# Norms walked by token halves: the third and fourth block ahead of each norm and the first two behind it, with all squares added on VectorE

## The chip, the cores and the metric

One core of a Trainium2 chip runs the whole program. The metric is the device time of one execution in microseconds (us). PE is TensorE, ACT ScalarE, DVE VectorE, POOL GpSimd, SP the engine whose queue issues the DMAs.

## What is computed

Two kinds of transformer layers in fp32: two layers of a first kind (attention with a pair of softmaxes, a pool mixer, a convolution, SwiGLU) and one layer of a second kind (latent attention beside a gated recurrence, SwiGLU). Each normalises 512 latent tokens and 256 context tokens of 1024 features before its input projection, and the residual again before its feed-forward part. For this case only this skeleton matters (cut from the reference):

```python
for l in range(DEPTH):                                   # 2
    h = modulate(rms_norm(x, norm1_g[l]), sh1, sc1)      # 512 tokens
    hc = modulate(rms_norm(xc, norm1_g[l]), csh1, csc1)  # 256 tokens
    ...
    x = x + g1 * jnp.einsum('blm,md->bld', mix, w_out[l])
    x = x + g2 * swiglu(modulate(rms_norm(x, norm2_g[l]), sh2, sc2), w_ffn_in[l], w_ffn_out[l])
    ...                                                  # xc likewise, in layer 0 only
# the second kind, one layer, on x and a new context ctx
h = modulate_2(rmsnorm(x, g_norm_mix[layer]), sh1, sc1)
hc = modulate_2(rmsnorm(ctx, g_norm_mix[layer]), csh1, csc1)
...
x = x + gt1 * mix_lat
x = x + gt2 * swiglu_2(modulate_2(rmsnorm(x, g_norm_ffn[layer]), sh2, sc2), w_gate[layer], w_up[layer], w_down[layer])
return rmsnorm(x, g_final)
```

with `rms_norm(x) = x * rsqrt(mean(x*x) + eps) * g` and `modulate(h) = h * (1 + scale) + shift`. The shifts, scales and gates come from a vector times w_mod.

## The kernel before

**Layout.** x lies in SBUF as 8 feature tiles of 128 partitions, each with 768 tokens (512 latent, then 256 context); layers 1 and 2 need only the 512 after their input projection. Every weight matrix is walked in blocks of 256 output columns, that is two output tiles. A block is numbered n through the whole program: per layer 10 or 14 input blocks (`base_in[l]`), 4 output blocks (`base_out[l]`), then the feed-forward part (`base_ffn[l]`) in groups of 6, 6, 6 and 4 up blocks, each group followed by 4 down blocks.

**A block.** SP loads its weights into one of two slots (`raw`, n % 2), once POOL has split block n-2. ACT copies the high part (`split_hi`, 1.9 us for 8 tiles), once PE is through with block n-2, and POOL subtracts to get the low part (`split_lo`, some 5 us, semaphore `lo_ready`). PE then makes three products per feature tile (high by high, high by low, low by high) of 128 x 128 weights with 512 tokens, and again with 256 context tokens in layer 0. Block n writes one half of PSUM, n % 2. For one block behind each norm there is a third place for the weights (`early_hi`, `early_lo`, 7 of its 8 tiles), so that its split needn't wait for PE.

**A norm.** There are seven, numbered ni = 0 to 6: before the input projection (even) and before the feed-forward part (odd) of layers 0, 1 and 2, and the final one (6). Norms 0, 2 and 4 are over 768 tokens, 1 too, the others over 512. Around norms 1 to 6 the four blocks ahead (output or last down blocks) add to x: DVE adds a tile's products (`add_to_x`), ACT squares the tile (`norm_square`), DVE adds the square to `n_acc` (`norm_add`, `NORM_ADDED` = 5 of them; the last two squares are summed by PE). PE then sums over the partitions by products with a column of ones (`token_columns`), ACT takes the root, DVE inverts it and spreads it to `n_wide`, PE transposes that into PSUM. Then tile by tile: DVE multiplies (`xg`), ACT adds the shift and rounds to the high part (`h_hi`), DVE makes the low part (`h_lo`, semaphore `n_h`). The first block behind the norm takes its 8 feature tiles in that order, waiting for each.

**Other work in between.** Modulation vectors are made in 12 pairs per layer, spread over earlier blocks (`place`, `pair_in_block`): 8 or 16 steps on DVE (`pair_halves`, half before the block's own work and half in the block before), then sums or transposes on PE at the end of the block (`then` in `products`, lines 2494 and 2507), and SP loads the next pair when one is saved. Each engine's order is the order written in its function; nothing is planned at run time.

The lines behind the steps: 2542 are the products of most blocks, 1162 and 1182 those of layer 2's input projection, 684 the column sums, 2483 a norm's transposes, 2836 those of the output, 2151 makes `xg`, 2138 `h_lo`, 1855 `h_hi`, 1788 splits the high part, 1680 the low part, 2174 a modulation step.

## Time and profile before

| | |
|---|---|
| median of 3 runs | 2583.73 us (2577.93 to 2584.11) |
| profiled execution: its time / its span | 2577.28 us / 2575.5 us |
| PE busy, share of the span | 2445.3 us, 95% |
| DVE | 1337.2 us, 52% |
| ACT | 798.5 us, 31% |
| POOL | 884.9 us, 34% |
| mean granted clock of PE | 0.966 of full speed |

The profile is of one execution. A line of a timeline gives start and length in us, the engine, the line of the kernel, what is written and read, and in brackets how long the engine had stood idle and what released it. Matmuls are pipelined, so the distance of their starts tells the rate, not their length.

### The profile page before, as it was taken

To read this page: it belongs to the slowest core of one execution; us is meant where nothing else is said; L and a number is where in the kernel's file an instruction comes from. 1 tells how busy PE (TensorE), PEld (TensorE's weight loads), DVE (VectorE), ACT (ScalarE), POOL (GpSimd) and SP (SyncE) were. 2 spreads that over 40 slices of the span, in tenths; PEclk is the share of its full clock that TensorE was granted. 3 is DMA by queue.
4 is the path that set the end of the run, shared out by engine and by line. 5 is a ranking of instruction groups with operands and counts; after the bars stand their busy time and mean duration, and the time that the engine had idled before them with its cause. 6 is when DMAs were issued, how large, how long until landed. Compare 5 with 4: busy or idle time off the path is not lost.

```text
span 2575.5 us, 30755 instructions
## 1 busy us (share of the span) xinstructions
PE 2445.3 (95%) x13017; PEld 2019.1 (78%) x13017; DVE 1337.2 (52%) x1709; ACT 798.5 (31%) x1088; POOL 884.9 (34%) x633
## 2 busy tenths in 40 slices
PE   7999899999999999899999999998999988999998
PEld 3888778788888888778777778877988557888886
DVE  2899766646444343695656655654562424211113
ACT  2222661311211111425732122235343443222222
POOL 2006002223333332365034445543453003454442
PEclk9898899899999999899999999998999999999999
DMA  8332203224334242232034546432113002233331
GB/s 265 95 104 83 66 1 111 70 87 143 99 113 132 82 131 82 65 107 75 1 98 131 149 146 175 151 115 66 50 35 114 17 1 65 70 95 98 90 98 58
DMA packets 309225, 240.57 MB, mean 93 GB/s; under 512 B 10692, under 2 KB 304831, under 8 KB 309087
## 3 DMA queue, kind: packets, MB, share of 16 engines
q1 hardware_dynamic: 308674, 238.47, 30.5%
q8 instruction: 103, 1.69, 0.3%
q14 instruction: 34, 0.28, 0.0%
q10 hardware_dynamic: 414, 0.13, 0.0%
HBM read 232.29 MB, written 2.10 MB: 91 GB/s over the span
## 4 chain that ended last, share of the span: by engine, by line
PE 86%; DVE 9%; ACT 3%; issue 1%; DMA 1%; POOL 0%; SPq 0%; DVEq 0%; ACTq 0%
PE ps L2542 62%; PE ps L1162 5%; DVE mod_w L2174 2%; PE ps L2577 2%; PE ps L946 2%; PE ps L684 2%; DVE mod_ctx L2174 1%; PE ps L733 1%; PE ps L1182 1%; PE ps L2457 1%; PE ps L2494 1%; PE ps L760 1%; DVE small L1050 1%; PE ps L908 1%; ACT probs L990 1%
## 5 line engine op out<-in xcount | busy, mean ns | idle before, releaser
L1680 POOL TENSOR_TENSOR w_lo<-raw,w_hi 128x512 fp32r<-128x512 f32 x518 | 757.2, 1492 | 1380.5 <-ACT w_hi L1788 1380.4
L2542 PE MATMUL ps<-h_hi,w_hi 128*128 128x512 f32 x1994 | 649.4, 372 | 25.2 <-DVE h_lo L2138 21.1
L2542 PE MATMUL ps<-h_lo,w_hi 128*128 128x512 f32 x1994 | 639.5, 367 | 0.0
L2542 PE MATMUL ps<-h_hi,w_lo 128*128 128x512 f32 x1994 | 638.9, 366 | 0.0
L1788 ACT ACTIVATE w_hi<-raw 128x2048 fp32r<-128x2048 f32 (+2 forms) x155 | 264.8, 1708 | 577.3 <-PE ps L2542 365.3
L2542 PEld LDWEIGHTS ps<-h_hi,w_hi 128*128 128x128 f32 x1994 | 340.4, 191 | 93.9 <-issue 23.1
L2542 PEld LDWEIGHTS ps<-h_hi,w_lo 128*128 128x128 f32 x1994 | 339.9, 190 | 67.1
L2542 PEld LDWEIGHTS ps<-h_lo,w_hi 128*128 128x128 f32 x1994 | 340.4, 190 | 65.9 <-issue 0.2
L2065 ACT ACTIVATE xg<-ps 128x512 f32<-128x512 f32 (+1 forms) x66 | 44.2, 670 | 679.4 <-PE ps L2542 492.6
L2174 DVE SCALAR_TENSOR_TENSOR mod_w<-mod_w,cond 128x512 f32<-128x512 f32 x224 | 242.0, 1080 | 3.4
L2542 PE MATMUL ps<-hid_hi,w_hi 128*128 128x512 f32 x704 | 231.7, 370 | 0.0
L2542 PE MATMUL ps<-hid_lo,w_hi 128*128 128x512 f32 x704 | 230.3, 368 | 0.0
L2542 PE MATMUL ps<-hid_hi,w_lo 128*128 128x512 f32 x704 | 230.3, 368 | 0.0
L2423 DVE TENSOR_TENSOR sq<-xg,ps 128x512 f32<-128x512 f32 (+1 forms) x66 | 51.1, 775 | 342.6 <-ACT xg L2065 342.5
L2201 DVE SCALAR_TENSOR_TENSOR x<-ps,modc,x 128x512 f32<-128x512 f32 (+1 forms) x160 | 100.6, 678 | 208.1 <-PE ps L2542 208.1
L2542 PEld LDWEIGHTS ps<-hid_hi,w_lo 128*128 128x128 f32 x704 | 120.4, 188 | 24.6
L2542 PEld LDWEIGHTS ps<-hid_lo,w_hi 128*128 128x128 f32 x704 | 120.5, 188 | 24.3
L2542 PEld LDWEIGHTS ps<-hid_hi,w_hi 128*128 128x128 f32 x704 | 120.5, 188 | 24.0
L2426 DVE TENSOR_TENSOR hid_lo<-sq,hid_hi 128x512 fp32r<-128x512 f32 (+1 forms) x66 | 90.2, 1367 | 85.8 <-ACT hid_hi L2068 85.8
L1087 DVE SCALAR_TENSOR_TENSOR conv_acc<-u_conv,col_b,conv_acc 128x783 f32<-128x783 f32 (+1 forms) x120 | 123.6, 1030 | 4.2
L2174 DVE SCALAR_TENSOR_TENSOR mod_ctx<-mod_w,cond,mod_ctx 128x512 f32<-128x512 f32 x112 | 108.3, 967 | 0.0
L1162 PE MATMUL ps<-h_hi,w_hi 128*128 128x512 f32 (+1 forms) x196 | 73.3, 374 | 0.9 <-POOL w_lo L1680 0.9
(380 smaller groups left out, 3225.8 us busy)
## 6 DMA issues: line engine op xcount, KB each, us to landing
mod_w<-in_w_mod SPq DMA_DIRECT2D x72, 1024.0 KB, 9.6
raw<-in_w_ffn_in SPq DMA_DIRECT2D x88, 512.0 KB, 5.3
raw<-in_w_in SPq DMA_DIRECT2D x54, 512.0 KB, 4.9
raw<-in_w_ffn_out SPq DMA_DIRECT2D x48, 384.0 KB, 3.8
raw<-in_w_out SPq DMA_DIRECT2D x24, 512.0 KB, 4.6
raw<-in_w_gate SPq DMA_DIRECT2D x22, 512.0 KB, 4.0
raw<-in_w_up SPq DMA_DIRECT2D x22, 512.0 KB, 5.4
raw<-in_w_down SPq DMA_DIRECT2D x24, 384.0 KB, 3.8
```

What stands on the lines that cost most here:

```text
L684: ins = pe.matmul(ps[:, at + j:at + j + 1], square[:, P * j:P * j + P], ones[:, 0:1], start=first and j == 0, stop=last, skip_group_check= ...
L946: ins = pe.matmul(ps[:, PV2_AT:PV2_AT + 256], values(us[u]["k0"] // P + k, us[u]["h"]), probs_t[:, k, 256 * (j % 2):256 * (j % 2) + 256], ...
L1087: ins = dve.scalar_tensor_tensor(acc, frm, w, acc, ALU.mult, ALU.add)
L1162: ins = pe.matmul(ps[:, at:at + tw], weight, v[:, k, t0:t0 + tw], start=(k == 0 and r == 0), stop=(k == KD - 1 and r == 2))
L1680: ins = pool.tensor_tensor(w_lo[:, s, at:end], raw[:, s, at:end], w_hi[:, s, at:end].bitcast(F32), ALU.subtract)
L1788: act.activation(w_hi[:, s, 0:floats], raw[:, s, 0:floats], ACT.Copy).then_inc(hi_ready, 1)
L2174: ins = dve.scalar_tensor_tensor(to, w, by, to if step >= chains else mod_bias[:, :, :], ALU.mult, ALU.add)
L2201: ins = dve.scalar_tensor_tensor(xt, ps[:, at:at + tw], modc[:, l % 2, chunk + 2 * b + t, c:c + 1], xt, ALU.mult, ALU.add)
L2423: dve.tensor_tensor(ffn_h[:, s, 0:T], ffn_sg[:, s, 0:T], ps[:, 2048 * s + 1024:2048 * s + 1024 + T], ALU.mult).then_inc(psum_free[s], 1)
L2426: dve.tensor_tensor(hid_lo[:, i, 0:T], ffn_h[:, s, 0:T], hid_hi[:, i, 0:T].bitcast(F32), ALU.subtract).then_inc(f_lo, 1)
L2542: ins = pe.matmul(ps[0:m, at:at + tw], weight(part, k, cols), v[:, held[k] if held else k, t0:t0 + tw], start=(at_k == 0 and j == 0 and no ...
L2577: ins = pe.matmul(ps[:, first + width * t:first + width * (t + 1)], v[:, k, rows], w[:, k, :], start=(k == 0 and j == 0), stop=(k == KD - ...
```

## The change

For norms 1, 2, 3, 5 and 6 the tokens are divided in two halves: 512 and 256 where there are 768 (norms 1 and 2), 256 and 256 otherwise. The first two blocks ahead of the norm stay whole. PE walks the third and fourth in six parts and two: third block's half 0 (both output tiles), fourth block's half 0, fourth block's half 1, third block's half 1; the norm's sums and transposes of half 0 lie between the last parts. The first two blocks behind norms 1, 3 and 5 are walked half 0 of both, then half 1 of both. The sums of half 1 stand in the first block behind the fifth feature tile, for norm 2 too. DVE adds, squares are summed and tiles are made half by half in an order written out in `late_adds`. All 7 additions of squares are made on DVE, so that PE sums one column per 128 tokens instead of three.

Norm 4 is done differently: its 256 context tokens don't change in layer 1, so their half is squared, summed and normed within layer 1's last group of up blocks (`CTX_BLOCK` and the two behind it); the 512 latent tokens follow where the norm was, and PE starts layer 2 with the context tokens of its first two blocks. Norm 6's output is turned and stored in two halves.

The places that go with it: the early weight buffers are now whole and serve the first block behind norms 1, 2, 3 and 5 (before: the second; at norm 4 still the second); the second block's high split stands on ACT between two squares of half 1; layer 2's modulation pairs sit one block later; `pool_wt` moves into memory behind the early buffers and is cleared once more by POOL in layer 1.

```diff
-EARLY = 7 * 256
+EARLY = 2048
...
-        place([(2, p) for p in range(12)], [base_ffn[1] + 1 + 3 * p for p in range(12)])
+        place([(2, p) for p in range(12)], [base_ffn[1] + 2 + 3 * p for p in range(12)])
...
-        early_blocks = [n for l in range(3) for n in ([base_in[l] + 1] if l else []) + [base_ffn[l] + 1]]
-        NORM_ADDED = 5
+        early_blocks = [base_ffn[0], base_in[1], base_ffn[1], base_in[2] + 1, base_ffn[2]]
+        NORM_ADDED = 7
...
+        HALVES = {1: [(0, LAT), (LAT, CTX)], 2: [(0, LAT), (LAT, CTX)], 4: [(LAT, CTX), (0, LAT)]}
+        SPLIT = (1, 2, 3, 5, 6)
...
+        LATE = {(2, 0, 0): 1, (2, 0, 1): 2, (3, 0, 0): 3, (3, 0, 1): 4, (3, 1, 0): 5, (2, 1, 0): 6}
...
+        CTX_BLOCK = base_ffn[1] + 30
...
+            block_ready(n, 0, n // 2)
+            pe.wait_ge(n_h[0], KD * 4 + KD)
+            first_products(wh, wl, 0, 1024, LAT, CTX)
+            norm_sums(4, 1)
+            first_products(wh, wl, 1, 1024 + CTX, LAT, CTX)
+            pe.wait_ge(psum_free[1], (n + 1) // 2)
+            norm_turn(4, 1)
+            pe.wait_ge(lo_ready, n + 2)
+            for t in range(2):
+                ins = first_products(*early_views(n + 1, 256), t, CTX_FIRST_AT + CTX * t, LAT, CTX)
+            ins.then_inc(in_tile, 1)
+            first_products(wh, wl, None, 0, 0, LAT, lambda k: pe.wait_ge(n_h[1], KD * 3 + k + 1)).then_inc(gemm_done, 1)
             project(1, {})
...
+            def norm_square(ni, h, i):
+                first, end = half_range(ni, h)
+                if i == 0:
+                    for k in range(2):
+                        if ni - k > 0:
+                            act.wait_ge(n_ss[k], ni - k)
+                    to = n_acc[:, first:end]
                 else:
-                    if m >= 3:
-                        act.wait_ge(n_added, NORM_ADDED * ni + m - 2)
-                    to = sq[:, m % 2, 0:T]
-                act.activation(to, x[:, m, 0:T], ACT.Square).then_inc(n_sq, 1)
+                    if i >= 3:
+                        act.wait_ge(n_added[h], NORM_ADDED * (ni - h) + i - 2)
+                    to = sq[:, i % 2, first:end]
+                act.activation(to, x[:, tile_order(ni, h)[i], first:end], ACT.Square).then_inc(n_sq[h], 1)
...
+                act.wait_ge(psum_free[(n0 + b) % 2], freed(n0 + b) + 1)
+                for h in range(2) if ni in SPLIT else (1,):
+                    for i in (2 * b, 2 * b + 1):
+                        norm_square(ni, h, i)
             def last_blocks(ni, n0):
+                if ni == 4:
+                    for b in range(3):
+                        next_hi(n0 + b)
+                        squares_of_block(ni, n0, b)
+                    split_early_hi(n0 + 5)
+                    act.wait_ge(n_x, 1)
+                    norm_square(ni, 1, 6)
+                    act.wait_ge(psum_free[(n0 + 3) % 2], freed(n0 + 3) + 1)
+                    norm_square(ni, 1, 7)
+                    return
+                for b in range(2):
                     next_hi(n0 + b)
                     squares_of_block(ni, n0, b)
+                for t in range(2):
+                    act.wait_ge(late_added, late_base(ni) + LATE[2, 0, t])
+                    norm_square(ni, 0, 4 + t)
+                if n0 + 4 < blocks_used:
+                    split_early_hi(n0 + 4)
+                for t in range(2):
+                    act.wait_ge(late_added, late_base(ni) + LATE[3, 0, t])
+                    norm_square(ni, 0, 6 + t)
...
+            def norm(ni, n0=None):
+                if ni in (0, 4):
+                    norm_root(ni, ni // 4)
+                    for m in range(KD):
+                        norm_tile(ni, ni // 4, m)
+                    return
+                norm_root(ni, 0)
+                act.wait_ge(late_added, late_base(ni) + LATE[3, 1, 0])
+                norm_square(ni, 1, 4)
+                if n0 + 5 < blocks_used:
+                    act.wait_ge(gemm_done, n0 + 3)
+                    split_hi(n0 + 5, 1, block_floats(n0 + 5))
+                act.wait_ge(psum_free[1], freed(n0 + 3) + 1)
+                norm_square(ni, 1, 5)
+                for m in range(KD):
+                    if m == 4:
+                        act.wait_ge(late_added, late_base(ni) + LATE[2, 1, 0])
+                        norm_square(ni, 1, 6)
+                    if ni < 6:
+                        norm_tile(ni, 0, m)
+                act.wait_ge(psum_free[0], freed(n0 + 2) + 1)
+                norm_square(ni, 1, 7)
                 if ni == 6:
                     return
+                norm_root(ni, 1)
                 for m in range(KD):
+                    norm_tile(ni, 1, m)
+                if ni % 2:
+                    act.wait_ge(gemm_done, n0 + 4)
+                    split_hi(n0 + 6, 0, block_floats(n0 + 6))
...
+                        if n != base_ffn[l]:
+                            split_hi(n + 2, s, block_floats(n + 2))
...
+                        if n == CTX_BLOCK:
+                            for k in range(KD):
+                                norm_square(4, 0, k)
+                        if n == CTX_BLOCK + 1:
+                            norm_root(4, 0)
+                        if n == CTX_BLOCK + 2:
+                            for m in range(KD):
+                                norm_tile(4, 0, m)
                     if g0 + g < HID // P:
...
+            def late_adds(ni, n0, l, chunk, gain, mods_needed, pair=None):
+                def add(b, h, t):
+                    n, (t0, tw) = n0 + b, halves_of(ni)[h]
+                    c, at, m = 1 if t0 == LAT else 0, half_at(n, t, h), 2 * b + t
+                    if (b, h, t) in LATE:
+                        dve.wait_ge(late_done, late_base(ni) + LATE[b, h, t])
+                    else:
+                        dve.wait_ge(gemm_done, n0 + (3 if b == 3 else 4))
+                    xt = x[:, m, t0:t0 + tw]
+                    dve.scalar_tensor_tensor(xt, ps[:, at:at + tw], modc[:, l % 2, chunk + m, c:c + 1], xt, ALU.mult, ALU.add
+                                             ).then_inc(late_added if (b, h, t) in LATE else psum_free[n % 2], 1)
+                add(2, 0, 0)
+                add(2, 0, 1)
+                norm_add(ni, 0, 4)
+                add(3, 0, 0)
+                norm_add(ni, 0, 5)
+                add(3, 0, 1)
+                norm_add(ni, 0, 6)
+                norm_add(ni, 0, 7)
+                if pair:
+                    dve.wait_ge(late_pair, 1)
+                    pair_out(dve.tensor_copy, pair, pair_columns(n0 + 2))
+                if ni < 6:
+                    norm_gain(ni, gain, mods_needed)
+                norm_spread(ni, 0)
+                add(3, 1, 0)
+                norm_add(ni, 1, 4)
+                add(3, 1, 1)
+                norm_add(ni, 1, 5)
+                def first_tile():
+                    add(2, 1, 0)
+                    norm_add(ni, 1, 6)
+                norm_tiles(ni, 0, {4: first_tile})
+                add(2, 1, 1)
+                norm_add(ni, 1, 7)
+                norm_spread(ni, 1)
+                norm_tiles(ni, 1)
...
+            def norm_sums(ni, h):
+                first, end = half_range(ni, h)
+                pe.wait_ge(n_added[h], NORM_ADDED * (ni - h + 1))
+                token_columns(pe, sums_at(ni, h), n_acc[:, first:end], (end - first) // P, True, True).then_inc(n_ss[h], 1)
+            def norm_turn(ni, h):
+                first, end = (v // P for v in half_range(ni, h))
+                pe.wait_ge(n_spread[h], ni - h + 1)
+                for j in range(end - first):
+                    at = rstd_at(ni, h) + P * j
+                    ins = pe.transpose(ps[:, at:at + P], wide(ni)[:, j, :], ident)
+                ins.then_inc(n_turned[h], 1)
...
+            def late_blocks(ni, n0, k_tiles, hi, lo, order=None, held=None, pair=None):
+                two, three = n0 + 2, n0 + 3
+                sp_ = halves_of(ni)
+                def part(n, h, t):
+                    done = late_done if (n - n0, h, t) in LATE else gemm_done
+                    half_tile(n, k_tiles, hi, lo, t, h, sp_[h], order, held).then_inc(done, 1)
+                block_ready(two, 0, freed(two))
+                part(two, 0, 0)
+                part(two, 0, 1)
+                block_ready(three, 1, freed(three))
+                part(three, 0, 0)
+                part(three, 0, 1)
+                if pair:
+                    pair_sum(pair, pair_columns(two)).then_inc(late_pair, 1)
+                part(three, 1, 0)
+                norm_sums(ni, 0)
+                part(three, 1, 1)
+                norm_turn(ni, 0)
+                if pair:
+                    pe.wait_ge(mod_saved, pairs_saved(pair))
+                part(two, 1, 0)
+                part(two, 1, 1)
+            def first_blocks(ni, n):
+                sp_ = halves_of(ni)
+                def ready(h):
+                    return lambda k: pe.wait_ge(n_h[h], KD * (ni - h) + k + 1)
+                pe.wait_ge(lo_ready, n + 1)
+                pe.wait_ge(late_added, late_base(ni) + LATE[2, 0, 1])
+                half_tile(n, KD, h_hi, h_lo, None, 0, sp_[0], None, None, ready(0), {4: lambda: norm_sums(ni, 1)})
+                norm_turn(ni, 1)
+                pe.wait_ge(lo_ready, n + 2)
+                pe.wait_ge(late_added, late_base(ni) + LATE[3, 0, 1])
+                for t in range(2):
+                    half_tile(n + 1, KD, h_hi, h_lo, t, 0, sp_[0])
+                pe.wait_ge(psum_free[0], freed(n))
+                half_tile(n, KD, h_hi, h_lo, None, 1, sp_[1], None, None, ready(1)).then_inc(gemm_done, 1)
+                pe.wait_ge(psum_free[1], freed(n + 1))
+                for t in range(2):
+                    ins = half_tile(n + 1, KD, h_hi, h_lo, t, 1, sp_[1])
...
+            pe.wait_ge(n_xg[0], KD * 6 + KD)
+            turn_out(0)
+            turn_out(1)
+            norm_sums(6, 1)
+            turn_out(2)
+            turn_out(3)
+            norm_turn(6, 1)
+            pe.wait_ge(n_xg[1], KD * 5 + KD)
+            for t in range(4, 8):
+                turn_out(t)
```

## Rows read from the trace of the kernel before

**Rows 1.** The chain that ended last, from part 4 of the page: share of the span by engine.

```profile
PE 86%; DVE 9%; ACT 3%; issue 1%; DMA 1%; POOL 0%; SPq 0%; DVEq 0%; ACTq 0%
```

**Rows 2.** Timeline of PE, norm 3: start, us, engine line op operands xcount [idle <-releaser].

```profile
1332.58 0.95 PE L684 MATMUL ps<-const,n_acc 128*128 128x1 f32 x8
1337.55 1.09 PE L2483 MATMUL ps<-const,n_wide 128*128 128x128 f32 x4 [2.24 <-DVE n_wide L2131]
1341.14 0.77 PE L2542 MATMUL ps<-h_hi,w_hi 128*128 128x512 f32 x1 [2.50 <-DVE h_lo L2138]
1341.70 0.63 PE L2542 MATMUL ps<-h_lo,w_hi 128*128 128x512 f32 x1
1342.13 0.63 PE L2542 MATMUL ps<-h_hi,w_lo 128*128 128x512 f32 x1
1347.46 0.40 PE L2542 MATMUL ps<-h_hi,w_hi 128*128 128x512 f32 x1
```

**Rows 3.** Timeline of PE: column sums and first product at norms 1, 2, 4 and 5.

```profile
456.23 1.39 PE L684 MATMUL ps<-const,n_acc 128*128 128x1 f32 x12
468.33 0.98 PE L2542 MATMUL ps<-h_hi,w_hi 128*128 128x512 f32 x2 [3.65 <-DVE h_lo L2138]
...
1044.98 1.47 PE L684 MATMUL ps<-const,n_acc 128*128 128x1 f32 x12 [0.29 <-DVE n_acc L2111]
1057.87 0.77 PE L2542 MATMUL ps<-h_hi,w_hi 128*128 128x512 f32 x1 [3.66 <-DVE h_lo L2138]
...
1736.89 1.47 PE L684 MATMUL ps<-const,n_acc 128*128 128x1 f32 x12 [1.90 <-DVE n_acc L2111]
1749.38 0.98 PE L2542 MATMUL ps<-h_hi,w_hi 128*128 128x512 f32 x2 [3.66 <-DVE h_lo L2138]
...
2175.18 0.95 PE L684 MATMUL ps<-const,n_acc 128*128 128x1 f32 x8
2183.73 0.77 PE L2542 MATMUL ps<-h_hi,w_hi 128*128 128x512 f32 x1 [2.50 <-DVE h_lo L2138]
```

**Rows 4.** Busy time by windows, line 1182: length, PE busy, PEld busy, clock, DMA, GB/s.

```profile
1797.00:1806.00 9.00, 8.73 (x75) 8.92 (x76) 1.00 0.36 116
```

**Rows 5.** Timeline of PE: products in pairs, 512 and 256 wide.

```profile
454.11 0.52 PE L2542 MATMUL ps<-h_hi,w_hi 128*128 128x512 f32 x2
454.46 0.52 PE L2542 MATMUL ps<-h_lo,w_hi 128*128 128x512 f32 x2
```

**Rows 6.** Timeline of DVE and ACT around norm 3.

```profile
1341.03 0.75 DVE L2151 SCALAR_TENSOR_TENSOR xg<-x,gscale,ps 128x512 f32<-128x512 f32 x1
1342.47 0.75 DVE L2151 SCALAR_TENSOR_TENSOR xg<-x,gscale,ps 128x512 f32<-128x512 f32 x1
...
1322.35 1.92 ACT L1788 ACTIVATE w_hi<-raw 128x2048 fp32r<-128x2048 f32 x1 [8.18 <-DMA raw<-in_w_ffn_in]
```

**Rows 7.** Timeline of DVE: a modulation step beside a working POOL, and one alone.

```profile
492.54 1.78 DVE L2174 SCALAR_TENSOR_TENSOR mod_ctx<-mod_w,cond,mod_ctx 128x512 f32<-128x512 f32 x1
...
498.30 0.74 DVE L2174 SCALAR_TENSOR_TENSOR mod_ctx<-mod_w,cond,mod_ctx 128x512 f32<-128x512 f32 x1
```

**Rows 8.** PE: group of a pair's transposes (lines view), and two waits there (timeline).

```profile
L2507 PE MATMUL ps<-const,mod_w 128*128 128x128 f32 x80 | 14.4, 284 | 9.8 <-DVE mod_w L2174 9.8
...
1404.46 0.33 PE L2507 MATMUL ps<-const,mod_w 128*128 128x128 f32 x1 [1.60 <-DVE mod_w L2174]
...
1436.73 0.47 PE L2507 MATMUL ps<-const,mod_w 128*128 128x128 f32 x1 [3.19 <-DVE mod_w L2174]
```

**Rows 9.** Timeline of PE: first column sums of a modulation pair, after feed-forward block 1.

```profile
504.57 0.28 PE L2494 MATMUL ps<-const,mod_w 128*128 128x1 f32 x2
```

**Rows 10.** Timeline of POOL: the low part of layer 2's first weight block.

```profile
1731.43 6.44 POOL L1680 TENSOR_TENSOR w_lo<-raw,w_hi 128x512 fp32r<-128x512 f32 x4 [3.10 <-ACT w_hi L1788]
```

**Rows 11.** Timeline of PE: sums of the two last tiles of squares, norm 0.

```profile
62.67 4.26 PE L684 MATMUL ps<-const,sq 128*128 128x1 f32 x24
```

**Rows 12.** Timeline of PE: the output's transposes.

```profile
2565.34 6.46 PE L2836 MATMUL ps<-const,x 128*128 128x128 f32 x32 [5.45 <-DVE x L2145]
```

443 lines of the change are left out of this document (245 added, 198 removed).

## Prediction

> **What bounds the kernel now.** I read the chain of waits first: 86% of it is PE [rows 1]. So time comes off only where PE stands or runs slow. Among the groups of instructions by line, PE stands longest before the first products and the transposes of the seven norms, so I read its timeline there. At norm 3 the last product ends at 1332.58, column sums follow, then transposes (after 2.24 us of waiting), and the next product starts at 1341.14: 8.6 us. The products that follow start 0.43 us apart until about 1347, and 0.23 us from there on: 14 at half clock cost 2.7 us more [rows 2]. Norm 3 costs 11.3 us. The same reading of rows 3 gives norm 1: 12.1 us, and 2.3 at half clock, 14.4; norm 2: 13.4, and 5.0 in which the first block waits tile by tile for DVE, 18.4; norm 4: 14.4 and 1.8, 16.2; norm 5: 8.6 and 1.5, 10.1 [rows 3]. These five, 70 us, are the most that halves can win.
>
> **The change, part by part.** *Width.* Halves turn products of 512 columns into twice as many of 256. In the stretch where only 256-wide products run there are 75 in 9 us, 0.12 us each [rows 4]; a pair of 512 and 256 takes 0.35 [rows 5], so 512 alone takes 0.23. Splitting costs nothing here. The Trainium skill (TensorE: Matmul & The Clock Gate, Back-to-back issue gap) gives sustained spacings of 81 ns at 128 columns and 131 ns at 512; between them, 256 would be near 98 ns, and two of them half as dear again as one of 512. By that, an estimate from the page, the 192 products split at each of norms 3 and 5 would cost some 20 us more each time, and nothing would be left to win. The trace disagrees in the stretch of rows 4, where a product of 256 takes half of one of 512.
>
> *The order of work, with norm 5 as the example.* t=0 is the start of the third output block; before, 22.4 us of products follow, then 10.1 lost, then 22.4: 54.9 us until the second feed-forward block ends. In the new order a half of a tile is 24 products, 2.8 us. PE does four of them (11.1), a fifth (13.9), the sums of half 0 (0.3), a sixth (16.9), four transposes' worth of turning (0.5), two more: free at 22.9. Beside this DVE and ACT must finish half 0. DVE adds, ACT squares, DVE sums: that chain, 0.45 us a step for 256 columns (my estimate, a little over half of 0.75 [rows 6]), keeps up to 16.9. Then ACT waits for the sixth part and, in front of the next square, splits a weight block: 1.9 us [rows 6], until 18.8. DVE's tiles of half 0 stand behind that square, and start at 20.1. POOL splits the same block from 18.8 on, and a DVE step with both operands in SBUF takes 1.78 us beside it, 0.74 alone [rows 7]; so the first tile is ready at 22.1. PE starts at 22.9 and is paced by DVE: 1.44 us a tile at 512 columns [rows 6], 0.85 at 256, and 1.3 once for the additions put in after tile 4. After its fifth tile (27.9) PE has the sums of half 1. They need all seven additions of that half, and DVE makes the last after the last tile of half 0: at 31.0. **Here a new wait of 3.1 us stands in the middle of a block**; behind it are three ready tiles. Then 2.1, the turn, and three half blocks of 5.5: 50.5. Does such a wait drop the clock? After 1.60 us it did not, after 3.19 us it did (that transpose took 0.47 us instead of 0.33) [rows 8], and nine products at half rate and the transposes cost 2.9. I take 2.5 here; bounds 0 and 2.9. Norm 5: 53.0, **2 us won**.
>
> *Norm 3* is the same, but ACT reaches the split for the early buffer at 7 and the block lands at 12.1, since ACT waits there for the DMA in the trace too [rows 6]; the squares of tiles 6 and 7 stand behind it, and everything is 2 us later: **1.2 won** against 11.3 lost before.
>
> *Norm 1* (halves 512 and 256, 5.6 and 2.8 us a half tile). PE is free at 36.8, the first tile is there at 38.2, PE does five until 46.9, the last addition comes at 50.7: a wait of 3.8, and the clock. Both blocks end at 80.5. But block 1 carries a modulation pair. Its second eight steps on DVE come after block 0's results, which now arrive only 5.5 us before block 1 ends instead of 17; eight steps, 0.7 each, and the 9.4 us for silu, product and split put the pair at 84.3. In the trace its sums start at 504.57, 84.2 us after the third output block's start, with no wait [rows 9]. **Nothing won.**
>
> *Norm 2* (512 and 256, but the next block needs only the 512). PE waits 1.5 at the sums of half 0, is free at 19.9, waits for the first tile until 23.2 (the split's 1.9 us and POOL again), and for half 1's sums from 31.9 to 35.6. It is through at 43.1 with the clock; before 17.0+13.4+16.2=46.6. **3.5 won.**
>
> *Norm 4.* The 256 context tokens are normed three blocks earlier. Their ACT and DVE work (8 squares, 7 additions, 8 tiles, some 11 us on DVE) goes into blocks of 11.2 us in which DVE has 4 to 6 of work; I cost it at 0.8 on PE, and 6 if that cover is short. Then PE has three context tiles, 8.7 us of products, to do while the other 512 are normed. POOL's low part of that block ends at 1737.9 [rows 10], 2.9 us after the last product, so PE waits for that first. Block 0 then ends at 29.0 and block 1 at 40.2 after the last product, before at 50.2; less the 0.8 and the later pair: **9 won**.
>
> *Norm 0*: 24 column sums less, 4.3 us [rows 11]; two additions more on DVE delay the first modulation copy by 0.8: **3.4 won**. *Norm 6*: DVE's scaling and the turning of the output go in halves; last product to end is 20.7 us now, of which 5.45 is one wait [rows 12]. Walked through, **0.9 won**, since four tiles still end the kernel.
>
> *Moved pairs.* Layer 2's modulation pairs move one block on. PE stands 9.8 us in all before such transposes now, the longest time 3.19 [rows 8]; the same eight or sixteen DVE steps meet the same POOL work one block later. Taken as 0, bounds -6 and +8. pool_w's new place costs nothing: its load waits for a clearing that POOL does a block earlier than it is read. SP's queue keeps its order; only the pair loaded behind (0, 9) is issued 6 us later, and is needed 30 us after that.
>
> Sum: 3.4+0+3.5+1.2+9+2.0+0.9 = 20 us. The profiled execution took 2577.28 (span 2575.5), so 2557.3 for one like it; the median is 6.45 above that execution, so 2583.7-20.1 = **2563.6**.
>
> **The rivals.**
> *The waits are shorter than I walk them.* If POOL does not slow the tiles and the last addition comes in time, the four inner waits (3.1, 3.1, 3.8 and 3.7, 13.7; of norm 1's some stays under its pair, so 13) and four clock losses (10) go too: 43 won, 2541. For it: all these come from chains of half-microsecond steps that I estimate. Against: DVE's order of instructions puts the last addition behind the last tile, whatever the durations.
> *The clock stays low from the first short wait to the last.* Then the five tiles ahead of the inner wait run at 0.43 a product: 5.6 us each at norms 1 and 2, 2.1 each at 3 and 5, 15 in sum, and 2579: the halves overlap, and little is won. For it: at norm 2 PE waits 3.3 before its first tile. Against: after 3.19 us the clock was back within ten products. The Trainium skill (TensorE: Matmul & The Clock Gate, HAM oscillation) tells of just this, short pieces of work between waits that each start at half clock; the rows show it only after the longer wait.
> *Slower: DVE becomes the bound in layer 1's feed-forward part.* If the moved double pairs fall beside POOL's splits, where a step takes 1.78 instead of 0.74, each of the four waits reaches 3.2 us and drops the clock, 6.1 each, 24.4 instead of 10.1 (1.6, 1.6, 3.2 and 0.8 us in the timeline and one clock loss), 14 more; with eight single pairs at 2 us each instead of 2.6 in sum, another 13: 2591. It decides from about four steps beside POOL in a block. For it: the waits are there already, and context work joins them. Against: one place did that in the trace, three double pairs did not.
>
> *Width costs after all.* If two 256-wide products took 0.35 us where one of 512 takes 0.23, the 192 split products at each of norms 3 and 5 would cost 22 us more, 45 in sum: 2608. Against: the 75 in 9 us.
>
> **How the numbers follow.** The walk as told 0.52 (2550 to 2573), shorter waits 0.22, the clock 0.15, DVE the bound 0.09, width 0.02. A measurement of this kernel tells 0.3%, 7.8 us, from no change. Faster by that: the first two and a little of the third, 0.76; within: 0.13; slower: 0.11. The low end takes in the second case, 2538; the high end the third, 2580.
>
> **What would show it.** At norms 1, 2, 3 and 5 the timeline of PE should show one wait of 3 to 4 us before column sums inside the first block, released by DVE's addition, and half clock behind it; at norm 4 a wait of some 3 us for POOL's w_lo, and none at the transposes; after feed-forward block 1 of layer 0 a wait of about 4 for modulation steps. No waits there: the second case. Products 0.43 apart ahead of the sums: the third. Waits before L2507's transposes above 20 us in sum: the fourth.

## The result, and the profile after

The changed kernel takes 2588.7 us (median of 15 runs, 2586.4 to 2596.3) beside 2581.3 for the kernel before in the same runs: ratio 1.0036, 95% interval 1.0025 to 1.0046. By the ratio it is slower by 9 us, where I had forecast 20 less. The profiled execution took 2587.0 us, its span is 2585.2 (before: 2575.5), with a mean clock of 0.965 (before 0.966).

I read the same views as before. First the chain that ended last, from part 4 of the page of the changed kernel; it answers to [rows 1]:

```profile
PE 79%; DVE 13%; ACT 4%; issue 2%; POOL 1%; DMA 1%; SPq 0%; DVEq 0%; ACTq 0%
PE ps L2733 51%; PE ps L1216 5%; PE ps L2773 4%; DVE conv_acc L1137 3%; DVE mod_w L2352 2%; PE ps L2838 2%; DVE mod_ctx L2352 2%; PE ps L996 2%; PE ps L783 1%; PE ps L1236 1%; POOL w_lo L1741 1%; PE ps L2686 1%; DVE n_acc L2230 1%; PE ps L810 1%; PE ps L735 1%
```

DVE's share rose from 9% to 13%, and its largest entries are not norms: the taps of the convolution (conv_acc, 3%), which is not among the fifteen entries named for the kernel before, and the modulation steps (mod_w, mod_ctx). Where this happens is seen when PE's timeline of both traces is laid side by side. The table gives, for landmarks of PE or ACT, start times in the profiled executions:

| landmark | before | changed | changed - before |
|---|---|---|---|
| first product of layer 0 (norm 0) | 73.4 | 70.6 | -2.8 |
| third output block of layer 0 (norm 1 begins) | 420.5 | 415.8 | -4.8 |
| silu of layer 0's third feed-forward block (norm 1 is past) | 523.5 | 521.4 | -2.2 |
| end of layer 1's first block (norm 2 is past) | 1074.1 | 1068.9 | -5.2 |
| attention of layer 1: PE's first wait of 2.8 us for probabilities | 1214.0 | 1227.4 | **+13.3** |
| silu of layer 1's fifth feed-forward block (norm 3 is past) | 1405.6 | 1419.6 | +14.0 |
| layer 2, a product behind norm 4 | 1980.3 | 1986.7 | +6.4 |
| end of layer 2's second feed-forward block (norm 5 is past) | 2207.6 | 2216.4 | +8.7 |
| end of the span | 2575.5 | 2585.2 | +9.7 |

Up to layer 1 the change had won 5 us. Then **18.5 us are lost in one stretch, 140 us long before and 158 in the changed kernel, that the diff touches only at its start**: the input projection of layer 1 and what follows until the first probabilities. Norm 4 gives 8 us back; norms 3, 5 and 6 lose 1 to 2 each. The first two rows are to be read with care: the kernels below that have the same code up to there have their first product between 70.3 and 74.6, and issue the pair sums behind layer 0's first output block between 390.7 and 399.7. So I compare stretches inside one trace from here on.

PE's timeline of the changed kernel at norms 1 to 5 (columns as in [rows 2], and it answers to [rows 2] and [rows 3]):

```profile
465.57 0.61 PE L735 MATMUL ps<-const,n_acc 128*128 128x1 f32 x4 [3.40 <-DVE n_acc L2230]
497.96 0.59 PE L2686 MATMUL ps<-const,mod_w 128*128 128x1 f32 x2 [3.63 <-DVE mod_w L2352]
...
1054.55 0.77 PE L2733 MATMUL ps<-h_hi,early_hi 128*128 128x512 f32 x1 [8.55 <-DVE x L2304]
1064.29 0.50 PE L735 MATMUL ps<-const,n_acc 128*128 128x1 f32 x4
...
1358.52 1.02 PE L735 MATMUL ps<-const,n_acc 128*128 128x1 f32 x4 [2.83 <-DVE n_acc L2230]
...
1755.17 0.39 PE L1314 MATMUL ps<-h_hi,w_hi 128*128 128x256 f32 x1 [2.40 <-POOL w_lo L1741]
...
2167.00 0.38 PE L2773 MATMUL ps<-h_hi,w_hi 128*128 128x256 f32 x1 [2.19 <-POOL w_lo L1741]
2190.51 0.38 PE L2773 MATMUL ps<-h_hi,early_hi 128*128 128x256 f32 x1 [1.12 <-DVE h_lo L2269]
2194.30 1.01 PE L735 MATMUL ps<-const,n_acc 128*128 128x1 f32 x4 [2.82 <-DVE n_acc L2230]
```

The inner waits before the second half's sums are there as walked at norms 1, 3 and 5 (3.40, 2.83, 2.82; forecast 3.8, 3.1, 3.1); at norm 2, where 3.7 were forecast, the sums at 1064.29 waited for nothing. As walked are also the wait for the modulation pair at norm 1 (3.63) and the wait for POOL at norm 4 (2.40; forecast 2.9). New to me are the wait of 8.55 at norm 2, and one of 2.2 for POOL's low part in the middle of the output projection at norms 3 and 5 (2.18 and 2.19).

Then the stretch that lost 18.5 us. PE and ACT of the changed kernel at the end of the input projection, then its DVE, then the same lines of DVE, ACT and PE in the kernel before:

```profile
1150.04 1.96 PE L2929 MATMUL ps<-conv_acc,const 128*128 128x512 f32 x4 [2.26 <-DVE conv_acc L1137]
1163.85 1.84 PE L2897 MATMUL ps<-const,qk_sq 128*128 128x2 f32 x8 [6.57 <-issue]
1163.19 1.23 ACT L2115 ACTIVATE v_nat<-conv_acc 128x512 f32<-128x512 f32 x2 [18.79 <-DVE conv_acc L2487]
```

```profile
1069.36 0.87 DVE L2284 SCALAR_TENSOR_TENSOR xg<-x,gscale,ps 128x256 f32<-128x256 f32 x2 [3.74 <-PE ps L2675]
1079.97 0.69 DVE L2432 TENSOR_TENSOR u_conv<-u_conv,conv_acc 128x512 f32<-128x512 f32 x1 [2.93 <-ACT u_conv L2085]
1081.29 36.26 DVE L1137 SCALAR_TENSOR_TENSOR conv_acc<-u_conv,col_b,conv_acc 128x512 f32<-128x512 f32 x30
1118.77 31.12 DVE L1137 SCALAR_TENSOR_TENSOR conv_acc<-u_conv,col_b,conv_acc 128x512 f32<-128x512 f32 x30
1162.47 1.28 DVE L2487 SCALAR_TENSOR_TENSOR conv_acc<-ps,conv_acc 128x512 f32<-128x512 f32 x2
```

```profile
1079.15 32.67 DVE L1087 SCALAR_TENSOR_TENSOR conv_acc<-u_conv,col_b,conv_acc 128x512 f32<-128x512 f32 x30
1113.05 30.88 DVE L1087 SCALAR_TENSOR_TENSOR conv_acc<-u_conv,col_b,conv_acc 128x512 f32<-128x512 f32 x30
1156.45 1.27 DVE L2305 SCALAR_TENSOR_TENSOR conv_acc<-ps,conv_acc 128x512 f32<-128x512 f32 x2
1157.17 1.23 ACT L2014 ACTIVATE v_nat<-conv_acc 128x512 f32<-128x512 f32 x2 [9.24 <-DVE conv_acc L2305]
1151.14 1.88 PE L2666 MATMUL ps<-conv_acc,const 128*128 128x512 f32 x4
1158.15 0.95 PE L2634 MATMUL ps<-const,qk_sq 128*128 128x2 f32 x8
```

Two tiles of 31 taps each stand on DVE one behind the other, 66 us without a gap before and 70 in the changed kernel; behind them two rotations of q (12.6 us), and then the subtraction of the convolution's mean, the c_yc step (line 2487, before 2305). PE meets this chain twice. It sums the finished taps (line 2666 before, 2929 now), and then asks for the step: its next column sums, behind which the rest of the projection is queued, wait for it. Before, the taps ended at 1143.9 and PE came to them at 1151.14, with 7.3 us of room. But the step ended at 1157.7 and PE issued the sums behind it at 1158.15: **DVE and PE arrived within half a microsecond of each other**, and no wait was to be seen. In the changed kernel DVE is 6.0 us later, and PE, 5 us ahead at the end of norm 2, is earlier: hence 2.26 and 6.57 of waiting. The step's lateness has two parts. The taps start 2.1 us later. DVE itself stood idle for 2.93 us before them, for ACT's copy of the convolution's input, and on ACT that copy stands behind the tiles of norm 2's context half, which PE's transposes release only behind the first block (1069.36). And the first tile's taps take 3.6 us longer, because PE's lead and the later start bring one more of POOL's splits beside them: of the first tile's 30 steps on line 1137, 14 are long ones, 10 before. Busy time of DVE in two stretches of the changed kernel (columns: length, DVE busy and count, clock, DMA share, GB/s), the first with POOL splitting, the second without:

```profile
1089.00:1101.00 12.00, 11.75 (x8) 0.86 0.32 100
1102.00:1109.50 7.50, 7.14 (x11) 1.00 0.48 143
```

In the timeline a tap is 1.66 us long beside POOL and 0.75 alone, so four more long ones are the 3.6. Behind the wait PE is slow as well; here the windows of the changed kernel (columns: length, busy time and count of PE, PEld, DVE, ACT, POOL, clock, DMA share, GB/s):

```profile
1160.00:1170.00 10.00, 6.15 (x26) 5.89 (x27) 3.72 (x4) 1.23 (x2) 6.01 (x8) 0.50 0.22 77
1170.00:1180.00 10.00, 10.00 (x42) 9.42 (x43) 0.00 (x0) 1.48 (x1) 0.00 (x0) 0.50 0.00 0
1180.00:1190.00 10.00, 10.00 (x88) 10.00 (x88) 6.83 (x5) 4.37 (x8) 9.42 (x5) 1.00 0.20 67
```

Between 1163.85 and about 1180 the granted clock is 0.5, the lower of its two levels (1.2 GHz): 16 us at half rate are 8 lost. 2.3 + 6.6 + 8, and 1.6 for a stretch at half clock around 1095, make the 18.5. That the waits brought the half clock with them is likely, but not shown (see the last section).

### The profile page after: what moved, and what is told of

Same layout as the page of the kernel before. It is cut to its first block, busy times and chain, and to the rows that moved or that the text cites. A ratio compares the mean times of both kernels' runs of the same rounds, so it can differ in the third digit from the quotient of the medians.

```text
span 2585.2 us, 31586 instructions
## 1 busy us (share of the span) xinstructions
PE 2435.1 (94%) x13305; PEld 2028.0 (78%) x13305; DVE 1385.8 (54%) x1829; ACT 816.3 (32%) x1155; POOL 881.5 (34%) x629
## 4 chain that ended last, share of the span: by engine, by line
PE 79%; DVE 13%; ACT 4%; issue 2%; POOL 1%; DMA 1%; SPq 0%; DVEq 0%; ACTq 0%
PE ps L2733 51%; PE ps L1216 5%; PE ps L2773 4%; DVE conv_acc L1137 3%; DVE mod_w L2352 2%; PE ps L2838 2%; DVE mod_ctx L2352 2%; PE ps L996 2%; PE ps L783 1%; PE ps L1236 1%; POOL w_lo L1741 1%; PE ps L2686 1%; DVE n_acc L2230 1%; PE ps L810 1%; PE ps L735 1%
## 5 line engine op out<-in xcount | busy, mean ns | idle before, releaser
L2733 PE MATMUL ps<-h_hi,w_hi 128*128 128x512 f32 x1760 | 573.1, 372 | 7.7 <-DVE h_lo L2269 3.7
L2733 PE MATMUL ps<-h_lo,w_hi 128*128 128x512 f32 x1760 | 564.2, 367 | 0.0
L2733 PE MATMUL ps<-h_hi,w_lo 128*128 128x512 f32 x1760 | 564.0, 366 | 0.0
L2733 PEld LDWEIGHTS ps<-h_hi,w_hi 128*128 128x128 f32 x1760 | 300.6, 191 | 65.2 <-issue 5.2
L2733 PEld LDWEIGHTS ps<-h_hi,w_lo 128*128 128x128 f32 x1760 | 299.9, 190 | 58.7
L2733 PEld LDWEIGHTS ps<-h_lo,w_hi 128*128 128x128 f32 x1760 | 300.3, 190 | 57.6 <-issue 0.2
L2733 PE MATMUL ps<-hid_hi,w_hi 128*128 128x512 f32 (+1 forms) x656 | 217.8, 372 | 0.0
L2733 PE MATMUL ps<-hid_lo,w_hi 128*128 128x512 f32 (+1 forms) x656 | 216.3, 369 | 0.0
L2733 PE MATMUL ps<-hid_hi,w_lo 128*128 128x512 f32 (+1 forms) x656 | 216.2, 369 | 0.0
L2230 DVE TENSOR_TENSOR n_acc<-n_acc,sq 128x256 f32<-128x256 f32 (+2 forms) x91 | 81.5, 903 | 29.7 <-ACT sq L1877 26.3
```

Of the source, the lines that this page charges most:

```text
L2230: dve.tensor_tensor(acc, acc, sq[:, i % 2, first:end], ALU.add).then_inc(n_added[h], 1)
L2733: ins = pe.matmul(ps[0:m, at:at + tw], weight(part, k, cols), v[:, held[k] if held else k, t0:t0 + tw], start=(at_k == 0 and j == 0 and no ...
```

## Experiments

The number to compare is the ratio to runs of the kernel before that were made beside each kernel's own; the changed kernel's is 1.0036 (1.0025 to 1.0046), and 0.001 is 2.6 us. Beside it I give the length of a stretch inside the trace, from the third of layer 0's last output blocks (norm 2 begins) to PE's first wait for probabilities in layer 1: 186.4 us before, 202.0 in the changed kernel.

### Is it DVE's chain? Fewer taps, in both kernels

```
 w = col_b[:, 62 * l + 2 * k + t:62 * l + 2 * k + t + 1]
+if l == 1 and k >= TAPS - 6:
+    width = 8
 frm, acc = u_conv[:, t, k:k + width], conv_acc[:, t, 0:width]
```

a_taps, in the changed kernel: 

> The changed kernel, with the last 6 of the 31 convolution taps of each of the two tiles of layer 1 working on 8 columns instead of 512 (so that part of the convolution is left out): 12 steps of about 1.05 us, some 12 us of DVE, are taken off the chain that ends at 1149.8. First theory: in layer 1 DVE's chain of taps sets the end of the input projection; PE's two new waits (2.26 at 1150.04, 6.57 at 1163.85) and the stretch at half clock until 1180 (about 8) go, 17 us less than the changed kernel: 2572, ratio to the kernel before 0.996. Rival: the loss sits in PE's own walk through norm 2 (its wait of 8.55 and the slow products behind), and the waits at 1150 and 1163 only pass it on: at most 2 us, 2587.

b_taps, in the kernel before: 

> The kernel before, with the same 12 taps of layer 1 cut to 8 columns. First theory: DVE's chain ended just in time there (ACT has the squares of the convolution at 1158, PE asks for them at 1158 to 1161), so nothing is won: 0 to 1 us, 2581, ratio 0.9996 to 1. If the chain already held PE up before, or if DVE's taps slow the rest of layer 1 by their mere presence, some 5 to 10 us are won: 2573.

Measured: a_taps 0.9996 (0.9987 to 1.0005), 10 us less than the changed kernel; b_taps 0.9997 (0.9985 to 1.001), nothing. The 12 shortened taps are worth 10 us in the one kernel and none in the other. (In the traces the two tiles of taps are 2.9 and 6.9 us shorter in a_taps, 3.2 and 3.1 in b_taps, so less DVE time was taken off in the kernel before; PE had no wait there to lose.) So the chain of taps bounds the changed kernel and did not bound the one before. The stretch fell from 202.0 to 190.2, not to the 185 that I expected, and the trace says why. PE's timeline of a_taps, and its windows:

```profile
1157.01 1.02 PE L2899 MATMUL ps<-const,qk_sq 128*128 128x2 f32 x8 [1.86 <-issue]
```

```profile
1150.00:1160.00 10.00, 8.14 (x54) 7.10 (x52) 6.87 (x5) 1.23 (x2) 9.45 (x8) 1.00 0.48 157
1160.00:1170.00 10.00, 10.00 (x44) 9.42 (x44) 0.00 (x0) 1.10 (x1) 3.30 (x4) 0.51 0.00 0
```

Of the wait 1.86 us are left, since the two rotations still stand ahead of the mean step, and this short wait is followed by 10 us at half clock with PE busy all the time. Together the wait and the half clock behind it are 7 us.

### What makes DVE late: the place of two steps of norm 2

a_turn moves the transposes of norm 2's context half into block 0, so that DVE gets them earlier:

```
-if l and b == 1:
-    pe.wait_ge(psum_free[0], n // 2)
-    norm_turn(2, 1)
...
-{4: lambda: norm_sums(2, 1)} if l and b == 0 else None
+{4: lambda: norm_sums(2, 1), 5: second_half_turn} if l and b == 0 else None
```

> The changed kernel, with the transposes of norm 2's context half put behind block 0's sixth tile instead of behind the whole block: DVE's tiles of that half can start at 1066.6 instead of 1069.4. First theory (DVE's order after norm 2 delays the taps): the taps start and end 2.7 us earlier, PE's wait of 2.26 goes and the one of 6.57 is 3.9, with a shorter stretch at half clock: 4 to 7 us less than the changed kernel, 2583. Rival (the loss is PE's own): 0, 2588.7.

a_turn_add also moves the addition for which PE waited 8.55 us:

```
-norm_tiles(ni, 0, {4: first_tile})
+norm_tiles(ni, 0, {0: lambda: add(2, 1, 0), 4: lambda: norm_add(ni, 1, 6)})   (norm 2 alone)
```

> As the run before, and DVE adds the context half of the fifth tile (the addition for which PE waits 8.55 us before layer 1's first product) behind its first tile of norm 2 instead of behind the fifth. PE's first product comes at 1050 instead of 1054.6; DVE's pace of 1.44 us a tile holds it from there, so block 0 ends 2 us earlier at most. First theory: the taps start no earlier than DVE's own tiles allow, 0 to 2 us less than the run before: 2582. If PE's late start is what costs: 4 us less and more, 2579.

Measured: a_turn 1.0047 (1.0032 to 1.0062), no gain; a_turn_add 1.0031 (1.0018 to 1.0044), no gain that can be told from the changed kernel. In the traces the stretch is 199.5 and 195.8 instead of 202.0, so 2.5 and 6.2 us were won there; neither shows in the medians, and the first is inside what the runs scatter. The waits of a_turn show why it was so little:

```profile
1152.85 1.96 PE L2929 MATMUL ps<-conv_acc,const 128*128 128x512 f32 x4 [1.19 <-DVE conv_acc L1137]
1166.64 1.84 PE L2897 MATMUL ps<-const,qk_sq 128*128 128x2 f32 x8 [6.55 <-issue]
```

PE is held by the taps at the first of these lines. From there it has 7.2 us of work to the second, and DVE has 13.8: two rotations and the step. **As long as PE waits at the first line, whatever is won ahead of the taps moves both, and the second wait stays at 6.55.** I had expected 3.9 there, and had not seen this. In a_turn_add PE no longer waits at the first line, and the second wait is 2.25.

### The step itself: the mean ahead of the second rotation

```
 rotate(0)
-if l:
-    inverse(1)
-    rotate(1)
 dve.wait_ge(c_sum, l + 1)
 ...                                  (the c_yc step)
+if l:
+    inverse(1)
+    rotate(1)
```

a_yc: 

> The changed kernel, with one step of DVE's order in layer 1 moved: the subtraction of the convolution's mean (the c_yc step, 1.3 us), for whose squares PE waits 6.57 us at 1163.85, stands ahead of the second rotation (6.6 us) instead of behind it. First theory: taps end at 1149.8, first rotation at 1156, the step at 1157.3, squares at 1158.5; PE asks at 1157.1, so 6.57 becomes 1.5 or less, and with it goes part or all of the half clock until 1180 (8): 5 to 14 us less than the changed kernel, 2578. The wait of 2.26 stays. Rival (the taps themselves are what is late, and the wait only moves behind the rotation, to the products of the scores): less than 2 us.

b_yc, the same in the kernel before: 

> The kernel before, with the same step moved. It had no wait there, so nothing is won; DVE idles some 3 us for PE's sums (1151.14), and the second rotation ends 3 us later. Theory: 0 to 1 us either way, ratio 1.000. If the second rotation has no spare time, 3 us more and a clock loss: 2585.

a_yc_ta, together with the two moves above: 

> Three edits together: the moved mean step, the early transposes of norm 2's context half and the early addition for which PE waited 8.55 us. Theory: the taps start some 4 to 5 us earlier, PE waits neither at 1150 nor at 1163: 16 to 20 us less than the changed kernel, 2571, ratio to the kernel before 0.996. Rival: PE is bound by its own work there, no less than the moved mean step alone.

Measured: a_yc 1.0018 (1.0005 to 1.003), 5 us less than the changed kernel (the two intervals just overlap), stretch 191.9; b_yc 0.9998 (0.9982 to 1.0014), nothing; a_yc_ta 0.9986 (0.9973 to 0.9998), **13 us less than the changed kernel and faster than the one before**, stretch 183.5. In a_yc the wait of 6.57 is gone and the one for the taps is left, 3.53 now. In a_yc_ta both are gone, and so is the half clock (its windows, to compare with those of the changed kernel above):

```profile
1150.00:1160.00 10.00, 10.00 (x70) 9.13 (x69) 9.52 (x7) 1.23 (x2) 9.53 (x7) 1.00 0.49 159
1160.00:1170.00 10.00, 10.00 (x84) 9.87 (x84) 5.38 (x4) 5.22 (x7) 9.02 (x8) 1.00 0.12 43
```

No work was removed; three steps stand elsewhere. In its profiled execution the stretch is 18.5 us shorter than in the changed kernel, all that had been lost there, and 2.9 shorter than before, close to the 3.5 forecast for norm 2; the medians give 13 of the 18.5, and where the rest went isn't shown. So the loss came from an order on DVE that had been just good enough.

### The halves of norms 1, 3 and 5

a_sums7 tests the inner wait that the prediction named:

```
-half_tile(n, ..., None, 0, sp_[0], None, None, ready(0), {4: lambda: norm_sums(ni, 1)})
-norm_turn(ni, 1)
+half_tile(n, ..., None, 0, sp_[0], None, None, ready(0))
+norm_sums(ni, 1)
...
-for t in range(2):
-    half_tile(n + 1, KD, h_hi, h_lo, t, 0, sp_[0])
+half_tile(n + 1, KD, h_hi, h_lo, 0, 0, sp_[0])
+norm_turn(ni, 1)
+half_tile(n + 1, KD, h_hi, h_lo, 1, 0, sp_[0])
```

> The changed kernel, with the column sums of the second half at norms 1, 3 and 5 behind all eight tiles of the first feed-forward block's first half instead of behind the fifth, and the transposes behind the next half tile (another 2.8 us). Theory: three tiles (2.1 us at norms 3 and 5, 4 at norm 1) cover the inner waits of 2.83, 2.83 and 3.40; 0.7 us is left of each, and the half clock behind them goes: 2.5 to 4 us each at norms 3 and 5; at norm 1 what is won goes into the wait of 3.63 for the modulation pair. In sum 5 to 8 less than the changed kernel, 2582. Rival (the second half's tiles now come too late, and the wait moves to its first product): no gain.

a_later moves one place of the modulation pairs, `place([(0, 10), (0, 11)], [base_ffn[0] + b for b in (1, 3)])` to `(2, 4)`: 

> The changed kernel, with only the modulation pairs (0, 10) and (0, 11) moved one feed-forward block on. Theory: the wait of 3.63 at 497.96 and the half clock behind it (some 2.7 us until block 2 ends) go, 6 less than the changed kernel, 2583; the inner wait of 3.40 stays. Rival (DVE has no room in block 2 either): the wait comes at block 2's end, no gain.

Measured: a_sums7 1.0032 (1.0018 to 1.0046) and a_later 1.0026 (1.0016 to 1.0037), neither to be told from the changed kernel with certainty. The traces tell more. At norm 5, from the third output block to the end of feed-forward block 1, it is 54.9 us before, 57.1 in the changed kernel and 53.2 in a_sums7: 3.9 won, the inner wait is 0.32. At norm 1 the gain goes to the next bound, as expected: PE's wait for the pair behind block 1 grows from 3.63 to 8.95. At norm 3 likewise, from 2.82 to 5.28. First lines of these pairs in a_sums7:

```profile
500.89 0.59 PE L2686 MATMUL ps<-const,mod_w 128*128 128x1 f32 x2 [8.95 <-DVE mod_w L2352]
...
1395.68 0.48 PE L2699 MATMUL ps<-const,mod_w 128*128 128x128 f32 x1 [5.28 <-DVE mod_w L2352]
```

In a_later the stretch from the third output block of layer 0 to the silu of feed-forward block 2 is 99.1 us; it is 103.0 before, 105.6 in the changed kernel and 105.2 in a_sums7. So the pair's wait and the half clock behind it were worth 6.5 us there, as expected; 4 of these are missing in the total. In the trace 3.5 are lost between PE's first wait for probabilities and the silu of layer 1's fifth feed-forward block, with the code unchanged there: 195.8 us, 192.3 in the changed kernel, 190.2 in a_yc. Why is open.

### All together

a_best: 

> The changed kernel, with the moved mean step, the early addition, norm 2's second sums behind block 0's seventh tile and their transposes behind its last, the late sums of norms 1, 3 and 5, and the pairs (0, 10) and (0, 11) one feed-forward block later (blocks 2 and 4 instead of 1 and 3). Theory: of the changed kernel's 2588.7 the mean step, the sums and the addition take 13 (the run of three edits), the late sums 3.8 at norm 5 and 2.5 at norm 3, and with the pair moved the 5 us at norm 1 are no longer eaten by a wait for modulation steps (8.95 behind block 1 with the late sums alone): 25 in sum, 2564, ratio to the kernel before 0.994. Rival (DVE is full around norm 1 and the wait only moves one block on): 2571.

a_best2: 

> As the run before, and layer 2's pairs one further block later (feed-forward blocks 3, 6, 9 of layer 1 and so on, instead of 2, 5, 8). Theory: with the late sums the first of them waited 5.28 us at 1395.68; a block later it waits about 2, so 3 us less than the run before, 2561. Rival: the waits of the later pairs grow by as much, no difference.

a_best3: 

> The combined kernel with the late sums, and of layer 2's pairs only the first one block later (feed-forward block 3 of layer 1; the others stay at 5, 8, 11 and so on). In the combined kernel that pair waits 5.30 at 1363.47. Theory: its wait falls to about 1.6, as it did with all pairs moved, and the later ones stay as they were: 3 to 4 less than the combined kernel, 2553. Rival: the wait goes to the next pair, no difference, 2556.

Measured: a_best 0.9912 (0.9894 to 0.9931), 2556.4 us, 32 less than the changed kernel where I expected 25; a_best2 0.9919 (0.9898 to 0.994), no different, as its rival said (PE's waits before the pairs' transposes are 15.2 us in sum, 13.4 in a_best); a_best3 0.9903 (0.989 to 0.9917), 2553.9 us, **1% faster than the kernel before** and 34 us than the changed one. Here two gains need each other: with the late sums and the moved pair the stretch at norm 1 is 92.1 us, 11 less than before, where each alone gave 105.2 and 99.1; it is 13.5 less than in the changed kernel, where the expectation had counted 5. PE's windows show it (columns: length, PE busy and count, clock, DMA share, GB/s), the changed kernel first, then a_best3 with its clock at 1 and no wait in the same stretch:

```profile
500.00:510.00 10.00, 10.00 (x41) 0.63 0.65 206
```

```profile
470.00:490.00 20.00, 20.00 (x141) 1.00 0.19 53
```

Moving the first of layer 2's pairs did what was expected of it, and what its rival said too: its wait fell from 5.30 to 1.64, and the next one's became 3.76 (0.17 in a_best); the sum is 13.2 instead of 13.4, and a_best3 can't be told from a_best by its time. In PE's timeline of a_best3:

```profile
1372.49 0.33 PE L2702 MATMUL ps<-const,mod_w 128*128 128x128 f32 x1 [1.64 <-DVE mod_w L2355]
1399.75 0.43 PE L2702 MATMUL ps<-const,mod_w 128*128 128x128 f32 x1 [3.76 <-DVE mod_w L2355]
```

There is no measurement of the halves with layer 2's pairs at their old places, since the transposes there would write to a PSUM bank that DVE still reads; so what their move alone cost or won isn't shown.

## Why the prediction was wrong

**The step that failed is the sum itself**: "norm 2: 3.5 won" was carried to the end as if PE set the pace behind it. The walk of norm 2 was close (46.5 us before, 43.1 forecast, 43.5 measured until block 0 ends), but 80 us further PE meets DVE, where DVE had just been in time: b_taps and b_yc show that before it cost nothing, and the two times 0.5 us apart show that it had no room either. I had read DVE's timeline at the norms and nowhere else. What I should have asked of each microsecond won: which other engine must also be earlier for PE to keep it? The convolution's taps were in the trace, 66 us without a gap, and the change moves the point where they start.

The rest, by the prediction's own steps:

- **Norm 0**, 3.4: 2.8 in the trace. Right.
- **Norm 1**, nothing: block 1 ends 78.6 us behind the third output block (80.5 forecast), the pair's wait is 3.63 as walked. Missed is the half clock behind that wait, which lasts until 507.4 (clock 0.63 from 500 to 510) and costs 4.7; the pair was ready 2.1 us sooner than walked, so 2.6 us are lost in all. I had costed the clock at the inner waits and not at this one.
- **Norm 2**: I forecast a wait of 3.3 before the first tile. It was 8.55, because layer 1's first block uses PSUM columns in which the context half of the fifth tile lies, and DVE adds that tile behind its fifth tile of the first half. I costed the added wait of the sums, and not this one. DVE's pace of the last tiles hid it: block 0 ended in time, though one long wait stood in the place of the two that I had walked (3.3 and 3.7), and that is luck. With the addition moved the two stand there, 2.91 and 2.43 us, and the stretch is 3.7 us shorter than in a_turn. PE's timeline of a_turn_add:

```profile
1054.02 0.47 PE L2736 MATMUL ps<-h_hi,early_hi 128*128 128x512 f32 x1 [2.91 <-DVE h_lo L2269]
1065.24 0.99 PE L735 MATMUL ps<-const,n_acc 128*128 128x1 f32 x4 [2.43 <-DVE n_acc L2230]
```

- **Norms 3 and 5**, 1.2 and 2.0 won: 0.7 and 2.3 lost. The inner wait and its clock were right. Missed: block 3 of the output projection is reached after half of block 2, 5.6 us, and ACT and POOL need 8 to split its weights behind block 1's end: 2.2 us of waiting at each, 1.2 at norm 6. I had walked this for norm 4's block alone. With the sums moved, norm 5 is 1.7 better than before: the forecast's 2.0 was in reach, with an order other than the one made.
- **Norm 4**, 9 won: 7.6 by the table, with its wait for POOL (2.40) and none at the transposes. The mechanism was right, but the number is close by luck. From the last product before the norm to the end of layer 2's second block it was 51.3 us and is 38.4 (forecast 50.2 and 40.2), 12.8 won. Ahead of it, in layer 1's feed-forward part, 3.7 are lost where 0.8 were allowed, 1.6 of them in longer waits before the pairs' transposes; behind it 1.4 are lost.
- **Norm 6**, 0.9 won: 1 lost. Behind the last product it is 1.4 shorter, though two waits of 3.56 and 3.32 stand where one of 5.45 had been [rows 12]; ahead of it 2.4 are lost, half of that in the wait of 1.20; half 0's sums and transposes stand there too now.
- **Moved pairs**, 0: the waits before the transposes are 10.9 us in sum, 9.8 before [rows 8]. Right within 1 us for the waits; the whole price of the move isn't shown.
- **Width**, 0: the products of 256 columns cost what half a product of 512 costs, also here: 24 in 2.8 us. (One sum in the prediction is off here: 192 products at 65 ns more, the difference of the spacings quoted there, are 12.5 us, not 20; it decides nothing, since the trace has the spacing itself.)

Without the 18.5 us the same execution would have ended at 2568.5, 11 us above the sum for it (2557.3). The terms fell short by 4.3 at norm 5, 2.6 at norm 1, 1.9 each at norms 3 and 6, 1.4 at norm 4 and 1.1 at norms 0 and 2, 13 in all, and 2 came back between norm 0 and norm 1, within the scatter there. So the small terms were too high by more than half of the gain, and the large loss was absent. My slower rival said the right engine at the wrong place: DVE as the bound, by pairs in layer 1's feed-forward part, with a chance of 0.09. The pairs waited there as before; the taps did it. The rival of the clock was wrong in its place too (the tiles ahead of the inner waits run at DVE's pace), and right in that the clock takes more than the waits: of the 18.5, 9.6 are half clock. The sum also started from a median of 3 runs, 2583.7; of 15 it is 2581.3, 2.4 us less.

## What to carry to other kernels

Before you add up gains on the bounding engine, list where it next meets each other engine, and how much time lies between the two arrivals there; a pair that meets within a microsecond without a wait is a second bound, and a gain ahead of it is kept only if both sides become earlier. A split in halves needs everything in its path to come in halves too: weights (the wait for POOL), additions (the inner wait), background work (the modulation pair); here each of these took the gain of the one before it, and only together did they give 1.3% against the changed kernel and 1% against the one before. If the order of a queue can be changed, look for the step that someone waits for, and put it ahead of those that nobody waits for yet: moving one step of 1.3 us was worth 5 us, with two more moves 13.

## What the runs showed of the hardware

**The clock does not follow the length of a wait.** After 1.86 us without work (a_taps) the clock was 0.51 for 10 us; after 2.40 (at 1755.17), 2.26 (at 1150.04) and 2.19 (at 2167.00) in the changed kernel the windows of the next 5 us have it at 1.00. The same wait for POOL, 3.15 us in one kernel and 3.10 in the other, was followed by no half clock before, and by half clock that cost 1.6 us after. PE busy and count, clock, DMA share and GB/s in the same window, the kernel before first:

```profile
1090.00:1100.00 10.00, 6.85 (x30) 1.00 0.34 107
```

```profile
1090.00:1100.00 10.00, 6.90 (x24) 0.83 0.34 106
```

And in a_yc the clock fell while PE had been busy for some 15 us (all engines' columns as above):

```profile
1160.00:1165.00 5.00, 5.00 (x35) 4.50 (x34) 5.00 (x6) 1.23 (x2) 4.84 (x3) 1.00 0.70 228
...
1170.00:1175.00 5.00, 5.00 (x22) 4.71 (x22) 0.96 (x2) 3.08 (x4) 1.68 (x2) 0.50 0.00 0
```

The stretch is the one whose products alternate with column sums of one or two columns, and it is also the one that stayed at half clock for 16 us in the changed kernel and for 10 in a_taps, with PE at 100% busy; in the kernel before it ran at 1.00 throughout. Four of the kernels waited where it begins, 6.57 us (changed), 6.55 (a_turn), 2.25 (a_turn_add) and 1.86 (a_taps), and ran at half clock for 16, 18, 17 and 10 us behind it. But since a_yc fell to half clock there with no wait for 15 us, these runs don't show that the wait is what brings it on, nor what decides.

**DVE beside POOL**: a tap with both operands in SBUF is 1.66 us long beside POOL's splits and 0.75 alone, like the modulation steps of [rows 7]. The Trainium skill (SBUF — State Buffer, SBUF: two separate sides) says of these two engines that they share a pair of ports which one of them holds for a whole instruction while the other is blocked; the trace agrees in that such a tap takes over twice as long. It means that a faster PE can slow DVE: it brings POOL's next split forward, and with the taps starting later 14 of the first tile's 30 were long instead of 10.
